# A two-layer hybrid trunk: weight ring of twelve places that holds the attentions' working sets, expert sums kept in PSUM, gather of raw rows

## What is computed

```
for layer in range(2):
    if layer == 0:                       # stick-breaking attention
        h = h + stick_breaking(rms_norm(h, a_norm) @ a_w_qkv) @ a_w_o
    else:                                # window of 128 tokens, 16 query heads on 2 key heads
        k, v = split(rms_norm(h, kv_norm) @ kv_w); k = rope(k)
        q = rope(rms_norm(h, b_norm) @ b_w_q)
        h = h + window_attention(q, k, v, sinks) @ b_w_o
    xt = rms_norm(h, ffn_norm[layer])
    combine = top-2 experts of the top group, softmax shares
    for g in range(4):                   # 8 experts a group, w_gate, w_up: 1024 x 512, w_down: 512 x 1024
        a = silu(xt @ w_gate[g]) * (xt @ w_up[g])
        h = h + (a * combine[g]) @ w_down[g]
return rms_norm(h, final_norm)
```

## Time and profile before

| what | us |
|---|---|
| median of 3 runs | 1163.14 |
| lowest and highest | 1161.4, 1169.86 |
| the profiled execution | 1159.34 |
| its span | 1157.4 |
| TensorE busy in the span | 870.0 |
| VectorE, ScalarE, GpSimd busy | 208.7, 237.3, 18.4 |
| chain that ended last, DMA | 50% |
| chain that ended last, TensorE | 42% |

### The profile page before, as it was taken

One profiled execution on the slowest core, in us unless ns is written; L12 is line 12 of the kernel. 1 busy time (PEld: TensorE's weight loads), 2 busy tenths in 40 slices (PEclk: granted clock), 3 DMA queues, 4 the chain that ended last, 5 costly groups with the idle time before them and its releaser, 6 DMA issues.

```text
span 1157.4 us, 18602 instructions
## 1 busy us (share of the span) xinstructions
PE 870.0 (75%) x7870; PEld 480.2 (41%) x7870; DVE 208.7 (18%) x516; ACT 237.3 (21%) x547; POOL 18.4 (2%) x38
## 2 busy tenths in 40 slices
PE   8999998676667766775669998868765766586756
PEld 4788564243223422342235646434322432243323
DVE  1022331120012001110113522201110101120012
ACT  2165432012001200120012414102101120112011
POOL 0000000000000000000002000000000000000000
PEclk9999999989789978997899999989788988899689
DMA  9932169999999999999999715999999999999995
GB/s 386 429 123 87 59 241 409 427 428 430 428 428 430 428 428 429 429 428 429 429 427 425 292 73 216 429 425 431 428 428 429 429 428 427 431 428 428 430 426 225
DMA packets 30989, 432.78 MB, mean 374 GB/s; under 512 B 3440, under 2 KB 3568, under 8 KB 4592
## 3 DMA queue, kind: packets, MB, share of 16 engines
q1 hardware_dynamic: 30816, 431.85, 88.6%
q10 hardware_dynamic: 144, 0.52, 0.1%
HBM read 431.31 MB, written 1.05 MB: 374 GB/s over the span
## 4 chain that ended last, share of the span: by engine, by line
DMA 50%; PE 42%; ACT 3%; DVE 2%; issue 1%; DVEq 0%; ACTq 0%; SPq 0%; POOL 0%; POOLq 0%
DMA ring<-in_w_moe 49%; PE ps L1286 10%; PE ps L1274 5%; PE ps L1156 5%; PE ps L1141 5%; PE ps L1330 4%; PE ps L1262 3%; PE ps L1354 2%; PE ps L1116 2%; PE ps L1085 1%; ACT xT L652 1%; PE ps L1320 1%; PE ps L1235 1%; PE ps L1380 1%; PE ps L1417 1%
## 5 line engine op out<-in xcount | busy, mean ns | idle before, releaser
L1286 PE MATMUL ps<-ring,xT 128*32 128x256 f32 x4096 | 293.7, 438 | 164.4 <-DMA ring<-in_w_moe 157.9
L1286 PEld LDWEIGHTS ps<-ring,xT 128*32 128x32 f32 x4096 | 137.3, 122 | 310.7 <-DMA ring<-in_w_moe 205.8
L1330 PE MATMUL ps<-ring,scr 128*32 128x256 f32 x2048 | 147.5, 437 | 44.1 <-DMA ring<-in_w_moe 33.3
L1330 PEld LDWEIGHTS ps<-ring,scr 128*32 128x32 f32 x2048 | 72.9, 122 | 100.7 <-issue 36.4
L945 DVE TENSOR_TENSOR scr<-scr,ps 128x128 f32<-128x128 f32 x64 | 18.4, 288 | 508.2 <-ACT scr L660 508.2
L660 ACT ACTIVATE scr<-ps 128x128 f32<-128x128 f32 x64 | 17.8, 278 | 401.5 <-PE ps L1286 401.5
L952 DVE COPY scr<-ps 32x256 f32<-32x256 f32 x128 | 53.3, 416 | 229.5 <-PE ps L1330 228.6
L666 ACT ACTIVATE scr<-ps 32x256 f32<-32x256 f32 x128 | 48.2, 377 | 191.4 <-PE ps L1330 190.7
L1262 PE MATMUL ps<-scr 128*128 128x512 f32 x128 | 62.9, 624 | 8.2 <-ACT scr L666 8.2
L1274 PE MATMUL ps<-scr,xn 128*128 128x256 f32 x256 | 59.5, 386 | 9.7 <-DVE scr L929 9.7
L1141 PE MATMUL ps<-ring,oT 128*128 128x512 f32 x128 | 56.9, 596 | 0.0
(11 more groups left out here) (142 smaller groups left out, 509.2 us busy)
## 6 DMA issues: line engine op xcount, KB each, us to landing
ring<-in_w_moe SPq DMA_DIRECT2D x192, 2048.0 KB, 34.4
ring<-in_w_a SPq DMA_DIRECT2D x7, 2048.0 KB, 28.5
ring<-in_w_b SPq DMA_DIRECT2D x4, 2048.0 KB, 38.5
ring<-in_w_a SPq DMA_DIRECT2D x2, 1024.0 KB, 8.7
h<-in_x SPq DMA_DIRECT2D x2, 512.0 KB, 4.5
ring<-in_w_b SPq DMA_DIRECT2D x1, 1024.0 KB, 36.2
out<-xn SPq DMA_DIRECT2D x4, 256.0 KB, 2.1
par<-in_small SPq DMA_DIRECT2D x1, 768.0 KB, 15.5
```

The lines of the kernel that those rows point to most:

```text
L1286: last = MM(ps[CAP * j:CAP * (j + 1), e % 2, 0:2 * P].rearrange("p (u f) -> p u f", u=2), xg[:, kk, CAP * e:CAP * (e + 1)], w[:, :, k, P * ...
L1330: last = MM(ps[CAP * c:CAP * (c + 1), 2 + b, 0:256], hT[:, b, CAP * j:CAP * (j + 1)], w[:, j, 256 * c:256 * (c + 1)], start=j == 0, stop=j ...
```

## The change

The ring has twelve places. The lists `A_AT`, `B_AT` and `MOE_AT` say which place each slot gets, and `FREE_LAP` which count of `freed` the first twelve loads of the second expert layer wait for. Two places, 8 and 9, hold the first attention's working set, V rows and triangle constants, and then take expert slots; two others, 4 and 5, hold the second attention's working set, Q rows, angles and sinks. Places 10 and 11 are free from the start. `xn`, `scr` and `small` go. SP's queue loads the triangle constants, the angles and `fgain`.

Squares write their unread result elsewhere (to PSUM behind an attention). There is no `xn` of normalised rows: the gather reads `h`, and VectorE multiplies `selg` by the norm factor `ss[:, 2, t]`. After the gather `selg` is built again and multiplied by the shares, and expert 1 begins with its transposes.

Banks 0 to 3 of PSUM hold `h` during an expert layer: `start_sums` writes it there by a product with the identity, `combine` accumulates onto it. After the first layer ScalarE and VectorE copy the sums to `h`; at the end the square and the last multiply read them in PSUM. Gate/up and Y have one bank each (`B_GU`, `B_Y`) instead of two.

```diff
-RING = 9
+RING = 12
 SLOT = 4096
...
-WARM_ROUTE = (6, 3)
...
+SCR_A, SCR_B = 8, 4
+A_AT = (0, 1, 2, 3, 4, 5, 6, 7)
+B_AT = (10, 0, 1, 2, 3)
+MOE_AT = (2 * (10, 11, 0, 1, 2, 3, 4, 5, 8, 9, 6, 7), 2 * (8, 9, 6, 7, 10, 11, 0, 1, 4, 5, 2, 3))
...
+FREE_LAP = (9, 10, 11, 12, 13, 13, 14, 15, 16, 16, 17, 18)
...
-        xn = sb("xn", [P, T, D])
...
-        scr = sb("scr", [P, SCRATCH])
...
+        cut = cutter(ring[:, SCR_A:SCR_A + 2, :].rearrange("p b n -> p (b n)"), 2 * SLOT)
+        v_rows = cut(T * D).rearrange("p (t n) -> p t n", t=T)
...
+        tri = cut(N_TRI)
+        ntri, nones, strict, capc = (tri[:, P * i:P * (i + 1)] for i in range(4))
...
+        cut = cutter(ring[:, SCR_B:SCR_B + 2, :].rearrange("p b n -> p (b n)"), 2 * SLOT)
+        q_rows = cut(T * D).rearrange("p (t n) -> p t n", t=T)
...
+        angles_sinks = cut(N_ROPE)
+        sinks = angles_sinks[:, C_SINK:N_ROPE]
+        mxB, nmxB, sumB, esB = (cut(2 * PAIRS).rearrange("p (b m) -> p b m", b=2) for _ in range(4))
...
-        selw = cut(T * NE * CAP).rearrange("p (t n) -> p t n", t=T)
         selT = cut(2 * T * P).rearrange("p (q t n) -> p q t n", q=2, t=T)
-        sil = cut(2 * P).rearrange("p (b n) -> p b n", b=2)
-        hact = cut(2 * P).rearrange("p (b n) -> p b n", b=2)
...
+        fgain = ring[:, MOE_AT[1][12], 0:D]
+        flat_x = xT[:, :, :].rearrange("p k n -> p (k n)").rearrange("p (t n) -> p t n", t=T)
+        acc = ps[:, 0:4, :].rearrange("p (t h) n -> p t h n", t=T)
+        B_GU, B_Y, B_HT, B_SEL = 4, 5, 6, 7
+        B_XG = (B_SEL, B_Y)
...
-            sp_.dma_start(par[:, A_CONST:N_SMALL], small_in[:, A_CONST:N_SMALL]).then_inc(params_in, 16)
+            sp_.dma_start(tri, small_in[:, A_TRI:A_TRI + N_TRI]).then_inc(tri_in, 16)
+            sp_.dma_start(par[:, A_REST:N_FIXED], small_in[:, A_REST:N_FIXED]).then_inc(params_in, 16)
...
+                    used = s + 1
+                    if layer == 1:
+                        used = FREE_LAP[s] if isinstance(lit, int) and s < RING else s + 1 + N_B + 1
...
-                load(slot_b(i), w_b[i], its, N_A + i - RING + 1, KD * 256 if i == 0 else SLOT)
-            load_layer(1, its)
+                load(B_AT[i], w_b[i], its, MOE_AT[0].index(B_AT[i]) + 1, KD * 256 if i == 0 else SLOT)
+                if i == 2:
+                    sp_.wait_ge(freed, its * SLOTS_GROUP + MOE_AT[0].index(SCR_B + 1) + 1)
+                    sp_.dma_start(angles_sinks, small_in[:, A_ROPE:N_SMALL]).then_inc(rope_in, 16)
+            n2 = load_layer(1, its)
+            sp_.wait_ge(freed, sp_.snap((n1 + n2) * NG) * SLOTS_GROUP + N_B + 1 + 1)
+            sp_.dma_start(fgain, bc(final_norm.rearrange("(a n) -> a n", a=1), 0, P)
+                          ).then_inc(fgain_in, 16)
...
+            for _ in range(RING - N_A - 2):
+                pool.sem_inc(freed, 1)
...
+            pool.wait_ge(prepared, 1)
+            for i in range(2):
+                free(o_psum, PAIRS)
...
+            free(ob_psum, NCH)
...
+                rows = h[:, t, :]
+                if n == 4:
+                    sums_stand(act, t, its)
+                    rows = acc[:, t, :, :].rearrange("p h n -> p (h n)")
+                else:
+                    rows_stand(act, n, t)
+                if n in (1, 3) and t:
+                    act.wait_ge(squared, T * n + t)
+                unread = (v_rows[:, t, :], after_attention, q_rows[:, t, :], after_attention,
+                          flat_x[:, t, :])[n]
+                nc.scalar.activation(unread, rows, ACT.Square,
...
-                act.wait_ge(rstd_done, T * (2 + 2 * layer))
-                for t in range(T):
-                    nc.scalar.activation(xn[:, t, :], h[:, t, :], ACT.Copy, scale=ss[:, 2, t:t + 1]
-                                         ).then_inc(xn_done, 1)
...
+                        if e == 1:
+                            act.wait_ge(selt_psum, it + 1)
+                            nc.scalar.activation(selT.rearrange("p q t n -> p (q t n)"), ps[:, B_SEL, :],
+                                                 ACT.Copy).then_inc(selt_done, 1)
...
+                sums_stand(act, t, its)
+                nc.scalar.activation(h[:, t, 0:D // 2], acc[:, t, 0, :], ACT.Copy).then_inc(added[t], 1)
...
-            act.dma_start(fgain, bc(final_norm.rearrange("(a n) -> a n", a=1), 0, P)
-                          ).then_inc(fgain_in, 16)
...
-                def add_quad(it, q):
-                    for i in range(4):
-                        t, half = i // 2, i % 2
-                        r = slice(512 * half, 512 * (half + 1))
-                        dve.wait_ge(comb_psum, it * 8 + (4 * q + i + 1))
-                        V.tensor_tensor(h[:, t, r], h[:, t, r], ps[:, 6 + i % 2, :], ALU.add
-                                        ).then_inc(added[t], 1)
...
+                    def chosen_rows():
+                        for t in range(T):
+                            last = V.tensor_tensor(by_expert(selg[:, t, :]), bc(iota.unsqueeze(1), 1, NE),
+                                                   bc(rank[:, t, cols].unsqueeze(2), 2, CAP), ALU.is_equal)
+                        return last
+                    chosen_rows().then_inc(sel_done, 1)
+                    dve.wait_ge(sel_done, it * 2 + 1)
                     for t in range(T):
-                        last = V.tensor_tensor(selg[:, t, :].rearrange("p (e s) -> p e s", e=NE),
-                                               slots, bc(rank[:, t, cols].unsqueeze(2), 2, CAP),
-                                               ALU.is_equal)
+                        last = V.tensor_scalar(selg[:, t, :], selg[:, t, :], ss[:, 2, t:t + 1], None,
+                                               ALU.mult)
                     last.then_inc(selg_done, 1)
-                    dve.wait_ge(selg_done, it + 1)
+                    dve.wait_ge(xg_psum, it * KD + KD)
+                    chosen_rows().then_inc(sel_done, 1)
+                    dve.wait_ge(sel_done, it * 2 + 2)
                     for t in range(T):
-                        last = V.tensor_tensor(selw[:, t, :].rearrange("p (e s) -> p e s", e=NE),
-                                               selg[:, t, :].rearrange("p (e s) -> p e s", e=NE),
-                                               bc(tokw[:, t, cols].unsqueeze(2), 2, CAP),
-                                               ALU.mult)
+                        last = V.tensor_tensor(by_expert(selg[:, t, :]), by_expert(selg[:, t, :]),
+                                               bc(tokw[:, t, cols].unsqueeze(2), 2, CAP), ALU.mult)
                     last.then_inc(selw_done, 1)
...
+                sums_stand(dve, t, its)
+                V.tensor_copy(h[:, t, D // 2:D], acc[:, t, 1, :]).then_inc(added[t], 1)
...
-                    V.scalar_tensor_tensor(out=xn[:, t, r], in0=h[:, t, r], scalar=ss[:, 2, t:t + 1],
+                for half in range(2):
+                    r = slice(D // 2 * half, D // 2 * (half + 1))
+                    V.scalar_tensor_tensor(out=h[:, t, r], in0=acc[:, t, half, :], scalar=ss[:, 2, t:t + 1],
...
-                warm(7, WARM_ROUTE[0])
+                def start_sums(t):
+                    for half in range(2):
+                        MM(acc[:, t, half, :], ident, h[:, t, D // 2 * half:D // 2 * (half + 1)], start=True,
+                           stop=False, skip_group_check=True)
+                start_sums(0)
...
-                warm(7, WARM_ROUTE[1])
+                start_sums(1)
...
-                            pe.wait_ge(added[0], it * 4 + (2 * q + half + 1))
-                        elif q == 1:
-                            pe.wait_ge(added[1], it * 4 + (half + 1))
-                        MM(ps[:, 6 + i % 2, :], selT[:, q, t, :], yq[:, q, 512 * half:512 * (half + 1)],
-                           start=True, stop=True).then_inc(comb_psum, 1)
+                        MM(acc[:, t, half, :], selT[:, q, t, :], yq[:, 512 * half:512 * (half + 1)],
+                           start=False, stop=False, skip_group_check=True).then_inc(summed[t], 1)
...
-                                last = MM(ps[:, 6 + k % 2, 0:NE * CAP], xn[:, t, P * k:P * (k + 1)],
+                                last = MM(ps[:, B_XG[k % 2], 0:NE * CAP], h[:, t, P * k:P * (k + 1)],
...
+                        if e == 1:
+                            transpose_shares()
```

253 lines of the change are left out of this document (109 added, 144 removed).

## The result

The changed kernel takes **1130.03 us** (median of 4 runs, 1128.58 to 1130.43); the kernel before took 1162.32 on the same chip. The ratio is 0.971 (95% interval 0.967 to 0.974), a gain of 32.3 us against a forecast of 31.1. The profiled execution took 1130.43 us with a span of 1128.6.

A forecast was written before the change was run, and what follows sets the result against it. Transfers bound the expert layers, TensorE the attentions. Terms -29.4, -1.1, -0.8, +1.2 and -0.5 sum to -30.6 us, taking the profiled execution to 1128.7; its median, 3.8 us above, gives 1132.5, stated as 1132, range 1125 to 1144.

The forecast's parts named there:

- The number: Whole program: all terms together -30.6 us on the profiled execution, 1159.3 to 1128.7; median forecast 1132.
- The ring: Both expert layers: three more slots stored at the first gate/up half's end, 6 x 4.895 = -29.4 us.
- Twelve places full before G: First layer: twelfth slot lands by 157.8 us, 12.6 before the first expert's first gate/up half ends; second layer, 13 before.
- TensorE to spare: Expert layers: 6.8 us of work against 14.7 of transfers an expert; TensorE catches up at slot 22, then waits.
- G within 1 us of 170.4: First layer: the first expert's first gate/up half, which frees the first place, still ends within 1 us of 170.4.
- Norm factor, +0.6 a layer: Routing, both layers: multiplying `selg` by the norm factor before the gather adds 0.6 us each, +1.2 in all.
- The middle: -0.8, -0.5 and +0.6: Second attention and routing: earlier key/value projection -0.8 us, `fgain` off ScalarE -0.5, `selg` multiplies before the gather +0.6.
- The end, -1.1: Program's end: sums accumulated in PSUM spare the last VectorE add, so the second tile's square starts earlier, -1.1 us.
- Seeds that cost nothing: Routing: identity products starting the sums replace warm products; second pair ends at 163.9, before the gather's 164.11, costing 0.
- The fallen clock, 0.12: Rival, chance 0.12: clock falls in the routing, gather and first gate/up half double, 5.7 us a layer; 1143 us.
- Late places: Rival, chance 0.05: places freed too late for one to three slots a layer, 4.9 us each; 1137 to 1147.
- A stream that slows: Rival, chance 0.03: twelve queued transfers instead of nine slow the stream, 10 us per cent; 1182 us at 5%.

The follow-up runs named there:

- e2: Changed kernel with only nine instead of twelve expert slots loaded ahead of the first freed place, in both layers; 1159.49 us.
- e9: Changed kernel with five constant 512-column products added in experts 2 to 6 of each group, extra TensorE work in few instructions; 1134.66 us.
- e1: Changed kernel with only nine instead of twelve expert slots loaded ahead of the first freed place, in the first layer only; 1143.76 us.
- e8: Changed kernel with first-layer slots 6 to 11 all held until the whole output projection is through; 1140.45 us.
- e3: Changed kernel with eleven instead of twelve expert slots loaded ahead of the first freed place, in both layers; 1138.57 us.
- e11: Changed kernel run once more, without any change, as a base on the same chip; 1131.49 us.
- e12: Changed kernel with four constant products added at the start, behind the first tile's transposes; 1129.27 us.
- e6: Changed kernel with both pairs of seed products moved ahead of the router product; 1142.75 us.
- e4: Changed kernel with each gate/up product of experts 1 to 6 of every group issued twice; 1145.31 us.
- e5: Changed kernel with eight constant 256-column products behind the weights' wait of each gate/up half in experts 1 to 6; 1258.48 us.

## Why the prediction held, step by step

- **The number.** The forecast stood on the profiled execution, -30.6 us, and between the two profiled executions it is -28.8. That the medians' 32.3 comes so near to 31.1 is in part luck: 3.4 us of it are the medians' distance from those two executions. A part of that is likely the start, below, but only one execution of the kernel before was profiled.
- **The ring, -29.4.** Measured -14.4 and -15.0 between the stages, -29.5 by e2 against the changed kernel. The price of a slot is right to 2% (4.8 for 4.895), it adds up over places and layers, and nine full places at G instead of twelve cost what the arithmetic says.
- **Twelve places full before G.** Right, with less in hand than forecast. The twelfth slot was to land by 157.8, 12.6 us before G; transfers of the first layer end at about 163.3, 9.5 us before it. The places came free 1.6 us later (the output projection's last stretch starts at 139.7), and the last transfer moved at 180 to 410 GB/s over 156 to 163, not at 428. In the second layer it is 9.4 us instead of 13.
- **TensorE to spare.** Right: e9, and TensorE waits for weights first at 232.25, on slot 22 of the first group, as forecast. The stream had no hole after G beyond what it had.
- **G within 1 us of 170.4.** Wrong: 172.7. The routing's 0.65 of it was forecast. The other 1.7 us come from the first 40 us of the program, which the prediction did not look at: the second tile's transposes started 0.2 us later and took 1.97 us instead of 1.09, the value projection 28.26 instead of 27.63. The clock over 10 to 15 us was 0.66 in the changed kernel and 1.00 in the profile of before. It is no property of the change: e1 and e8, unchanged at that place, had 1.00 there and started the output projection at 137.8 and 137.7, as before at 138.0; the nine other executions with that code had 0.50 to 0.66 and started it at 139.4 to 141.4. For the same reason slot 22 and the second G came 2 us later than forecast (699.4 for 696.9).
- **Norm factor, +0.6 a layer.** Measured 0.62 and its hand-over, 0.65.
- **The middle: -0.8, -0.5 and +0.6.** Together -0.7; measured -0.4, and -0.7 in e1 to e3, e11 and e12 (114.4 us each). The 0.3 between them are the router product of the second routing, 4.06 us at the fallen clock. The angles and `fgain` made nobody wait.
- **The end, -1.1.** Measured -1.3.
- **Seeds that cost nothing.** Right in the sum, and here with a reason that the prediction did not have: they were costed at full clock and took 3.43 us at 0.50, and the ranks' wait for VectorE took that up. In eight of the twelve first routings they had the full clock and took 1.96. The second pair ended at 165.7, 0.75 us before the gather, and not at 163.9.
- **The fallen clock, 0.12.** The clock fell in some executions, but never in a first gather, and where it fell it cost 0 or 0.3 us. e6 shows that the rival's mechanism exists, and that its price is 2.5 us a layer, not 5.7, because the first gate/up half is at full clock again.
- **The other rivals.** Late places: there is a margin of some ten microseconds, and e8, 11 us past it, pays 9.9. A stream that slows: 426 to 432 GB/s in the slices of the expert layers with nine, eleven and twelve places.

What stays open: how a fetch holds up eight of a transfer's sixteen parts, if it does (0.2 us of e4's loss for each of 74 fetches); why TensorE pauses for 3.6 us in e9; why the clock falls in the routing in some executions and not in others; and why the second input tile comes at 10.0 in some executions and at 10.6 in others.

## What to carry to other kernels

Where stages bound by TensorE alternate with stages bound by transfers, a place in the ring is worth one slot's transfer for each change-over, if it is free early enough to be filled before the first consumer frees a place, and worth nothing more in the steady stream. Count the idle time of the queue just ahead of that instant: it says how many more places could pay (here ten microseconds, so two places by this arithmetic; no run has more than twelve), and whatever delays that instant is paid in full. Spare time of an engine should be measured by giving it work in few instructions; many instructions measure something else as well.

## What the runs showed of the hardware

- The clock fell to 0.50 while TensorE was continuously busy by the page. In e1 it fell at about 157.7, inside the router product's 32 records of 40 columns (154.44 to 158.5); in the changed kernel at about 160.3, just behind them (they end at 160.0), in the first records of 512 columns. It was 1.00 again from about 163.7 there, behind the first four records of 512 columns. The same code kept 1.00 throughout in eight of twelve first routings.
- At the start it stood at 0.66 over 10 to 15 us or lower behind pauses of 2.2 to 2.5 us in most executions, at 1.00 behind pauses of 1.55, 1.61 and 1.98; but once (e5) it was 0.66 behind 1.56, so the pause alone does not say. In both executions with records of 256 columns in the pause it was 1.00.
- Code was fetched in 21 or 22 pieces of 16 KB with 7850 TensorE records in the page, 22 with 8250, 83 with 9386 and 96 with 10922. Only TensorE's code differs between these kernels; what is fetched again starts somewhere between the second and the third.
- A transfer of 2 MiB lands in sixteen parts within 2.5 us of each other in the changed kernel and in e9. In e4, with 42 fetches a layer instead of 5 or 6, eight of the parts lag up to 10.2 us by the end of a layer.
